# dt's columns stream with V in three narrow blocks ahead of q and k, in a two-layer hybrid trunk on one core

## What is computed

```python
h = rms_norm(x, pre_mix_norm)
proj = h @ w_in                       # q, k, v, z 1024 columns each, xbc 1536, dt 16
attn = moba_attention(q, k, v)        # 8 heads of 128, rotary on 32 dims; causal in 256 tokens
xbc = silu(conv(xbc)); dt = softplus(dt + dt_bias)
y = ssd_scan(xs * dt, dt * a, B, C) + d_skip * xs
y = rms_norm(y * silu(z)) by group
x = x + rms_norm(concat(attn, y) @ w_out)
x = x + rms_norm(relu(rms_norm(x) @ w_up) ** 2 @ w_down)
```

## Time and profile before

| | us |
|---|---|
| median of 3 runs | 2171.31 (2171.27 to 2171.34) |
| the profiled execution | 2170.41 |
| its span, first to last instruction | 2168.7 |
| TensorE busy | 2156.5 (99%) |
| VectorE busy | 1375.2 (63%) |
| ScalarE busy | 1090.3 (50%) |
| mean granted clock of TensorE | 0.999 |

### The profile page before, as it was taken

One profiled execution on the slowest core, in us unless ns is written; L12 is line 12 of the kernel. 1 busy time (PEld: TensorE's weight loads), 2 busy tenths in 40 slices (PEclk: granted clock), 3 DMA queues, 4 the chain that ended last, 5 costly groups with the idle time before them and its releaser, 6 DMA issues.

```text
span 2168.7 us, 32398 instructions
## 1 busy us (share of the span) xinstructions
PE 2156.5 (99%) x11413; PEld 1854.8 (86%) x11413; DVE 1375.2 (63%) x1649; ACT 1090.3 (50%) x1658; POOL 109.7 (5%) x104
## 2 busy tenths in 40 slices
PE   9999999999999999999999999999999999999998
PEld 9888888888888888888898888888888888888887
DVE  7987565765565565456589975657555645554655
ACT  6554554653454454455465545556434534544543
POOL 2051000000000000000001410000000000000000
PEclk9999999999999999999999999999999999999999
DMA  7655565665666666665556555656666566656664
GB/s 230 180 151 175 156 198 180 204 193 195 194 191 194 191 189 195 192 193 193 182 152 194 157 164 161 198 175 201 203 192 192 182 204 180 204 194 193 177 208 149
DMA packets 232845, 404.35 MB, mean 186 GB/s; under 512 B 12508, under 2 KB 62452, under 8 KB 232244
## 3 DMA queue, kind: packets, MB, share of 16 engines
q1 hardware_dynamic: 231780, 398.57, 59.7%
q10 hardware_dynamic: 720, 4.26, 0.5%
q0 software_dynamic: 256, 0.33, 0.1%
HBM read 401.01 MB, written 2.10 MB: 186 GB/s over the span
## 4 chain that ended last, share of the span: by engine, by line
PE 99%; issue 0%; ACT 0%; DVE 0%; DMA 0%; POOL 0%; POOLq 0%; DVEq 0%; ACTq 0%
PE wide L1007 21%; PE wide L880 16%; PE wide L878 16%; PE wide L879 16%; PE wide L1015 11%; PE wide L954 8%; PE wide L961 4%; PE wide L929 1%; PE wide L931 1%; PE wide L1144 1%; PE wide L932 1%; PE wide L1046 1%; PE wide L1165 0%; PE wide L1182 0%; PE wide L1131 0%
## 5 line engine op out<-in xcount | busy, mean ns | idle before, releaser
L1365 DVE TENSOR_TENSOR w_lo<-raw,w_hi 128x1024 fp32r<-128x1024 f32 x752 | 927.3, 1242 | 687.4 <-ACT w_hi L571 645.4
L571 ACT ACTIVATE w_hi<-raw 128x1024 fp32r<-128x1024 f32 x752 | 789.1, 1053 | 501.5 <-PE wide L880 446.0
L878 PE MATMUL wide<-w_hi,u_hi 128*128 128x512 f32 x1280 | 498.5, 389 | 0.0
L880 PE MATMUL wide<-w_hi,u_lo 128*128 128x512 f32 x1280 | 498.0, 389 | 0.0
L879 PE MATMUL wide<-w_lo,u_hi 128*128 128x512 f32 x1280 | 497.9, 389 | 0.0
L1007 PE MATMUL wide<-a_both,w_hi 128*128 128x512 f32 x1778 | 425.2, 389 | 0.0
L1007 PEld LDWEIGHTS wide<-a_both,w_hi 128*128 128x128 f32 x1778 | 333.7, 188 | 64.1
L879 PEld LDWEIGHTS wide<-w_lo,u_hi 128*128 128x128 f32 x1280 | 240.3, 188 | 49.9
L880 PEld LDWEIGHTS wide<-w_hi,u_lo 128*128 128x128 f32 x1280 | 240.3, 188 | 49.7
L878 PEld LDWEIGHTS wide<-w_hi,u_hi 128*128 128x128 f32 x1280 | 240.3, 188 | 49.6
L1015 PEld LDWEIGHTS wide<-a_both,w_lo 128*128 128x128 f32 x2032 | 250.2, 188 | 10.7
(11 more groups left out here) (252 smaller groups left out, 1542.0 us busy)
## 6 DMA issues: line engine op xcount, KB each, us to landing
raw<-in_w_up SPq DMA_DIRECT2D x256, 512.0 KB, 3.9
raw<-in_w_down SPq DMA_DIRECT2D x256, 512.0 KB, 4.5
raw<-in_w_in SPq DMA_DIRECT2D x176, 512.0 KB, 3.8
raw<-in_w_out SPq DMA_DIRECT2D x64, 512.0 KB, 4.5
zg<-in_post_mix_norm ACTq DMA_DIRECT2D x2, 1024.0 KB, 4.9
zg<-in_post_mlp_norm ACTq DMA_DIRECT2D x2, 1024.0 KB, 8.3
out<-x_sb SPq DMA_DIRECT2D x8, 256.0 KB, 2.5
x_sb<-in_x SPq DMA_DIRECT2D x3, 512.0 KB, 8.9
```

The lines of the kernel that those rows point to most:

```text
L571: act.activation(w_hi[:, c % RING], raw[:, c % RING], ACT.Copy).then_inc(sem["hi_ready"], 1)
L878: pe.matmul(o, sh, wh, start=(k == 0 and not loaded), stop=False, skip_group_check=loaded)
L880: ins = pe.matmul(o, sl, wh, start=False, stop=(k == KT - 1), skip_group_check=loaded)
L1365: dve.tensor_tensor(lo[:, c % RING], raw[:, c % RING], hi[:, c % RING].bitcast(F32), ALU.subtract).then_inc(sem["split_done"], 1)
```

## The change

The order of the mixer's blocks becomes xBC 0 to 2, V 3 to 5, q and k 6 to 9, z 10 and 11, w_out 12 to 15: one block and eight slots more. V's 1024 columns are cut in three, at 240 and 640 in layer 0, at 496 and 768 in layer 1. dt's 16 columns are split by ScalarE and VectorE in pieces, beside the first V block's chunks, and are 16 further columns of its matmuls. The 32 matmuls of dt, its copy and its turn go; dt_inputs takes two steps, not four, reads the accumulators, and moves to slot 34; series, ends, skip pairs and the decay pair follow at 35 to 41, segments at 47 and on (before 38 and on), the rotary at 55 + 4r, scores behind 68 + 5p. Blocks 6 to 9 each hold one half of q heads and one half of k heads (two heads each), so that scores(p) needs two rotary steps more with each p. The copies w_last and w_first now have room of their own and serve block 1's first chunks as well. In V blocks whose matmuls are narrower than 512 columns the odd chunks go product by product over both token tiles instead of tile by tile. The third V block sums in acc[1], as does the first half of block 6 behind it, which waits for it; z uses the other pair of banks than b % 2 (side). w_out's chunks come in the order 4, 5, 0, 1, 2, 3, 6, 7.

```diff
-B_XBC, B_Q, B_K, B_V, B_Z, B_OUT, B_MLP = 0, 3, 5, 7, 9, 11, 15
+B_XBC, B_V, B_QK, B_Z, B_OUT, B_MLP = 0, 3, 6, 10, 12, 16
+HALVES = [1, 2, 6, 7, 8, 9]
+V_ENDS = [[0, 240, 640, 1024], [0, 496, 768, 1024]]
...
-PE_DT, PE_DT_TURN, PE_DECAY, PE_CB, PE_STATE = 7, 10, 17, 28, 31
+PE_INV, PE_DECAY, PE_CB, PE_STATE = 7, 37, 29, 43
-PE_SEG = [34 + 2 * i for i in range(8)]
-PE_YD = [38 + 2 * i for i in range(8)]
-PE_YOFF = [48, 52]
-PE_SCORE = [59 + 5 * p for p in range(4)]
+PE_SEG = [43 + 2 * i for i in range(8)]
+PE_YD = [47 + 2 * i for i in range(8)]
+PE_YOFF = [57, 61]
+PE_SCORE = [68 + 5 * p for p in range(4)]
...
-AD_DIAG, AD_DTT, AD_DT, AD_DECAY, AD_XDT, AD_CB, AD_STATE = 8, 11, 14, 21, 30, 32, 35
+AD_DIAG, AD_DT, AD_DECAY, AD_XDT, AD_CB, AD_STATE = 8, 34, 40, 41, 33, 47
-AD_SEG = [38 + 2 * i for i in range(8)]
-AD_Y = [44 + 4 * j for j in range(4)]
+AD_SEG = [47 + 2 * i for i in range(8)]
+AD_Y = [53 + 4 * j for j in range(4)]
-AD_SKIP = [28, 29, 31, 32]
-AD_ROPE = [37, 39, 45, 47, 53, 55, 60, 62]
+AD_SKIP = [37, 38, 39, 40]
+AD_ROPE = [55 + 4 * r for r in range(8)]
+OUT_ORDER = [4, 5, 0, 1, 2, 3, 6, 7]
...
+                if is_v(b):
+                    n = v_cols(b)
+                    ins = act.activation(in_slot(w_hi, c, 0, n), in_slot(raw, c, 0, n), ACT.Copy)
+                    if b % NB == B_V:
+                        act.wait_ge(*upto("wdt_landed", b // NB, 16))
+                        ins = act.activation(in_slot(w_hi, c, n, SH), wdt[:, c * CK:(c + 1) * CK], ACT.Copy)
...
-                if up or type(b) is int and displaced(b % NB, c):
+                if up or type(b) is int and b % NB in HALVES:
...
+            def token_chunk(c, banks, s_hi, s_lo, tiles=range(TT), loaded=False, n=CB, order=range(NC)):
+                if n < CB and c % 2:
+                    for kk, p, t in itertools.product(range(CK), range(3), tiles):
+                        k = c * CK + kk
+                        weights = (s_lo if p == 2 else s_hi)[:, k, t * P:(t + 1) * P]
+                        moving = (w_lo if p == 1 else w_hi)[:, c % RING, kk * CB:kk * CB + n]
...
-                def inv_row_and_dt():
-                    pe.wait_ge(once["const_ready"], 6)
+                def inv_rows():
+                    pe.wait_ge(once["const_ready"], 5)
...
-                    for k in range(KT):
-                        w = wdt_both[:, k * 2 * SH:k * 2 * SH + P]
-                        pe.matmul(o, w, a_hi[:, k], start=(k == 0), stop=False)
-                        ins = pe.matmul(o, w, a_lo[:, k], start=False, stop=(k == KT - 1))
-                    ins.then_inc(sem["dt_mm"], 1)
...
-                            pe.wait_ge(*(half_left(l, b - 1, 0) if b > 1 else (acc_free[1], l * per_acc[1] + 2)))
+                            pe.wait_ge(*((acc_free[1], l * PER_ACC + 2) if b == 1 else left(l, B_V + 2, 2) if b == B_QK
+                                         else half_left(l, b - 1, 0)))
...
-                        for part in range(2):
-                            src = M[1][:, t * P + part * SH:t * P + (part + 1) * SH]
...
+                        link(dve.scalar_tensor_tensor(dts[:, DT_IN, t], acc[side(B_V)][t][:, n:n + SH],
+                                                      st[:, X_INV, t:t + 1], row[:, 0], ALU.mult, ALU.add))
```

More of the change, by code:

```diff
@@ L114 @@
 SQ_Y1 = SQ_X1 + TT * QB
-DVE_LINKS = 46
+DVE_LINKS = 44
 SHIFT, ROOM = 16, 128
@@ L206, in trunk, with is_v, v_cols, in_slot @@
         w_hi_off = w_hi
[L209 to L213, removed]
+        w_last, w_first = w_ends[:, 0:2], w_ends[:, 2:4]
+        def is_v(b):
+            return type(b) is int and B_V <= b % NB < B_QK
+        def v_cols(b):
+            i = b % NB - B_V
+            return V_ENDS[b // NB][i + 1] - V_ENDS[b // NB][i]
+        def in_slot(a, c, c0, n):
+            return a[:, c % RING].rearrange("p (k n) -> p k n", k=CK)[:, :, c0:c0 + n]
         qk = ybuf[:, :].rearrange("p (h s) -> p h s", s=SEQ)
@@ L292, in shifted @@
             if place < B_MLP:
-                off, first = 0 < place < B_V, place == 1
+                off, first = place in HALVES, place in (1, B_QK)
             else:
@@ L725, in _ @@
                             act.activation(probsT[:, 0:3 * P], M[1][:, 0:3 * P], ACT.Copy).then_inc(sem["pt_a"], 1)
-                    for i in range(2):
+                    for i in range(3):
                         if slot == leaves(B_V + i):
@@ L870, in take @@
                 pe.wait_ge(sem["split_done"], RING + 1 + chunk(b, c))
-            def token_chunk(c, banks, s_hi, s_lo, tiles=range(TT), loaded=False):
+            def token_chunk(c, banks, s_hi, s_lo, tiles=range(TT), loaded=False, n=CB, order=range(NC)):
[4 more added lines that the diff above has]
+                        moving = (w_lo if p == 1 else w_hi)[:, c % RING, kk * CB:kk * CB + n]
+                        ins = pe.matmul(banks[t][:, 0:n], weights, moving, start=False,
+                                        stop=(k == KT - 1 and p == 2))
+                    ins.then_inc(sem["mm_done"], 1)
+                    return
                 for kk, t in itertools.product(range(CK), tiles):
                     k = c * CK + kk
-                    wh, wl = (w[:, c % RING, kk * CB:(kk + 1) * CB] for w in (w_hi, w_lo))
-                    o = banks[t]
-                    sh, sl = (s[:, k, t * P:(t + 1) * P] for s in (s_hi, s_lo))
+                    wh, wl = (w[:, c % RING, kk * CB:kk * CB + n] for w in (w_hi, w_lo))
+                    o = banks[t][:, 0:n]
+                    sh, sl = (s[:, order[c] * CK + kk, t * P:(t + 1) * P] for s in (s_hi, s_lo))
                     pe.matmul(o, sh, wh, start=(k == 0 and not loaded), stop=False, skip_group_check=loaded)
@@ L1242, in _ @@
                         pe.wait_ge(*down_left(l, 1, 0, 0))
-                    if (b == 0 or b >= B_V) and (l or slot):
+                    if b not in HALVES and (l or slot):
                         take(l * NB + b, c)
@@ L1269, in _ @@
                         pe.wait_ge(once["prm_copied"], DEPTH)
-                    if slot == PE_DT:
-                        inv_row_and_dt()
-                    if slot == PE_DT_TURN:
-                        dt_turn()
+                    if slot == PE_INV:
+                        inv_rows()
                     if slot == PE_DECAY:
@@ L1738, in _ @@
                             to_lo("attnT", j + 1, j, ATTNT_BANK[j], G_ATTN)
-                    for i, k in itertools.product(range(1, B_V), range(2)):
+                    for i, k in itertools.product(HALVES, range(2)):
                         if slot == half_slot(i, k):
```

176 lines of the change are left out of this document (89 added, 87 removed).

## The result

The changed kernel takes 2176.57 us (median; 2175.66 to 2177.94) against 2171.27 us (2170.62 to 2171.6) for the kernel before, measured beside it: a ratio of 1.0025, with its 95% interval 1.0017 to 1.0033. Forecast were 2170.1 us and no change that can be told. The measured time is 6.5 us above that and 0.6 us beyond the upper end of the range, 2176.0.

A forecast was written before the change was run, and what follows sets the result against it. TensorE's stream was taken to bound the kernel: -7.5 (dt's matmuls) + 2.0 (narrow V) + 0 (accumulators) + 3.8 and 0.5 (waits for VectorE, layers 1 and 0) = -1.2 us, giving 2170.1 us; range 2164.9 to 2176.0.

The forecast's parts named there:

- dt's matmuls removed: TensorE: dt's 32 separate matmuls per layer go, 3.74 us per layer on the path, 7.5 us saved in all.
- V's narrow matmuls: TensorE in V: three blocks of narrower chunks replace two, +1.0 us per layer, +2.0 in all (+1.4 to +2.6).
- accumulators twice: TensorE before chunk 48: acc[1] is needed again, but work between hides ScalarE's copies; cost nothing, uncovered 1.0 us per layer.
- VectorE behind block 3, layer 1: Layer 1, chunks 36 to 42: TensorE waits for VectorE's late splits, 3.4 us plus 0.4 for GpSimd, 3.8 us.
- the same, layer 0, and its start: Layer 0: no wait beside dt's steps in chunks 35 on; 0.5 us around chunks 28 and 29 of narrow block 3.
- dt's turn, with the short pauses around it: TensorE: two transposes of dt, a tenth or two of a us per layer, left out against similar trifles.
- rival 3: VectorE, ScalarE: dt's steps later than summed, softmax and rope work stopping TensorE, or lost cover; 1 to 2 us each; chance 0.16.
- p = 117: V's matmuls: assumed ns between starts at 256 columns, taken between 113.8 and 120, giving 44.6 us per layer.
- the chain: VectorE in layer 1: dt's series, ends, skip pairs and decays delay splits for chunks 36 to 42; TensorE waits 3.4 us.
- Rival 1: V blocks: VectorE keeps up, so only TensorE's work counts; 2165.2 us, or 2166.4 with the slower pace; chance 0.26.
- rival 2: Narrow V blocks: the ring of four raw weight slots turns too slowly, with 6 us landings 2176.6 us; chance 0.12.
- Rival 4: Narrow V chunks: the alternating token-tile order does nothing, pace 120 ns; +0.6 us, inside the forecast, no chance of its own.

The follow-up runs named there:

- Run 1: Changed kernel with VectorE's rotary steps placed behind the softmax steps within each slot: 2172.44 us, ratio 1.0005.
- run 7: Changed kernel with the split activations a_both, and all declared behind them, laid 64 bytes further in memory: 2226.03 us, ratio 1.0252.
- run 8: Kernel before with w_lo's 64-byte offset (SHIFT) set to 0: 2187.55 us, ratio 1.0076.
- run 3: Changed kernel with all narrow V chunks tile by tile, without the alternating order: 2177.26 us, ratio 1.0028.
- run 5: Changed kernel with segment sums, y_diagonal, y_offset and their steps one slot later, so nothing stands between chunks 47 and 48: 2179.82 us, ratio 1.0042.
- run 4: Kernel before with 30 of dt's 32 matmuls per layer left out, so dt is wrong: 2167.09 us, ratio 0.9981.
- run 6: Changed kernel with seven of the twelve steps of dt's series left out, output wrong: 2174.12 us, ratio 1.0014.
- run 9: Changed kernel, V cut at 240 and 752 in both layers: 2173.71 us; also with rotary steps behind softmax: 2169.01; that with narrow chunks tile by tile: 2169.09.

## Why the prediction was wrong

Step by step, in us over both layers, from the distances of starts in the profiled runs:

| step of the sum | forecast | found |
|---|---|---|
| dt's matmuls removed | -7.5 | -7.5 |
| V's narrow matmuls | +2.0 | +3.6 |
| accumulators twice | 0 | 0 |
| VectorE behind block 3, layer 1 | +3.8 | +2.9 |
| the same, layer 0, and its start | +0.5 | +1.9 |
| values() behind the rotary steps | not in it | +5.0 |
| dt's turn, with the short pauses around it | left out | -0.5 |
| sum | -1.2 | +5.4 |

The profiled executions differ by 5.5 us (2170.41 and 2175.93).

- **Failed: the work that moved next to other work.** The prediction costed each moved piece by duration and put the softmax and rope pieces into rival 3 as a load ("some 90% of VectorE"), at 1 to 2 us. A load was the wrong view: 90% busy would have done. What counts is that in a slot of VectorE's program the rotary steps come first, and that the copy for values() stands behind 1.4 us of them, and once more behind a wait for GpSimd. Both slot lists and the order of the blocks stand in the code; comparing them would have given four waits. Run 1 shows the whole term: 5.0 us by distances of starts, 4.1 net in the time.
- **Mis-sized: the narrow pace.** The step "113.8 is half of 226.9, so the pace is 0.443 ns per column with next to no fixed part" compared two places in SBUF, not two widths (runs 7 and 8). Nor is 120 a limit that the order of the stationary operands sets: both orders have it (run 3). At one place the rows give N/2.4 + 13.3 ns, and V's work is 45.4 us per layer in place of 43.6: +1.8, where I took +1.0 from p = 117 and from 0.443 ns per column (177.3 for 400, which measured 180; 120.6 for 272, which measured 125.5). The bound of +2.6 for both layers was too low as well. The Trainium skill (TensorE: Matmul & The Clock Gate, Back-to-back issue gap), N/2.4 + 2.5 ns for a matmul by itself, has the right form and slope: from 400 to 512 columns the rows give 47 ns for 112 columns, 0.42 ns per column. Its fixed 2.5 ns is not what these fp32 matmuls show; they show 13.3.
- **Right: the chain.** VectorE's chain decides in layer 1, and the waits for w_lo stand before the chunks foretold, first 1.27 before chunk 36 (forecast 1.2), then 0.1 to 0.3 each. 2.9 in place of 3.8: the slower matmuls (125.5 in place of 120.6 ns) gave VectorE about 0.06 us per chunk, and the rest of the difference I can't place row by row. (The sum itself had a slip of 0.1: 17.9 - 14.6 is 3.3, not 3.4.) The Trainium skill (VectorE: DVE Perf Modes, The TRN2 errata) would make a step of 32 elements an estimated (32 + 151)/0.96 = 191 ns; the rows have 0.18 to 0.19 us for one, and 0.23 from start to start in the series. Its price for the splits, by which the wait would have been 0.7 us longer than the forecast, is further off than the rows' distances.
- **Layer 0** had waits of 0.66 us before chunk 36, where I had summed "no wait", and 0.3 around chunks 28 and 29, where I had 0.5; smaller ones make 1.3 in all. The chain is the same and the slots were forecast even (2.1 against 2.1), so a slip of this size was within their accuracy. The 0.66 is the low end: the variants that leave layer 0's V and the chain as they are show 0.7 to 1.4 there. The other 0.6 lie in waits that were already at the start of layer 0 before the change; the traces vary there by up to 1.0 us, and whether the change has any part in it stays open.
- **Right: the accumulators.** Nothing is waited for at chunk 48; the cover is 1.2 us per layer (run 5), forecast 1.0.
- **The removed work** came out in full, for a reason that the prediction did not give. Alone it is worth 4.0 of 7.0 us (run 4). In the changed kernel it pays fully, where the chain has left the slots that dt's matmuls had given time to; no run tests this link by itself.
- **Rivals.** Rival 1 did not happen, rival 2 is refuted (2.8 us landings, VectorE without a pause, run 6); that its 2176.6 us is the measured time is chance. Rival 4 is true (the paces of run 3, and run 9). The result is a rival 3 with one of its mishaps, larger than its price.

The chances, 0.16 for slower, followed from a too small price for rival 3: with its 5.0 us it would have stood beside the forecast, not behind it.

## What to carry to other kernels

Before moving work beside other work, write down for each slot what the bounding engine waits for and what stands ahead of it in the other engine's program; a share of busy time doesn't show this, and the cure (two blocks of code exchanged) cost nothing and gave 4.1 us. When tiles become narrower, count a fixed part per matmul, and take it from two widths with operands placed alike. When work is removed from the bounding engine, ask whose slack it was: here 3 of 7 us were.

## What the runs showed of the hardware that I had not expected

- The pace of a matmul changed with where its operands lie in SBUF. With 256 columns it is 120 ns where both lie alike, 113.8 where the stationary w_lo lies 64 bytes further, and mostly 118 where the moving activations do. With the activations off by 64 bytes, 512 columns take 230 to 233 ns in place of 227, 400 take 184 in place of 180. Moving a_both and all behind it cost 49.5 us, and taking w_lo's offset away 16.4, part of it in matmuls whose own operands had not moved (run 8). Only one offset was tried, and what makes it so stays open.
- With operands that lie alike, N/2.4 + 13.3 ns per matmul held at five widths within about 1 ns, whatever the order of the stationary operands.
- GpSimd's cosine product of 32x512 took 1.76 us at one place and 2.92 at another (217.74 and 232.59 in layer 0 of the changed kernel; the other two there took 2.9); what lay beside it to make the difference wasn't tested.
